# Regrouped first products, a second carrier for the sample-row writes, and waits with other releasers, in a two-layer decode step

## The chip, the cores and the metric

The kernel runs on one core of one Trainium2 chip. The metric is the device time of one execution in microseconds (us). TensorE (PE) multiplies and transposes, VectorE (DVE), ScalarE (ACT) and GpSimd (POOL) work on what it makes, and SyncE (SP) issues most transfers. ACT and POOL can issue transfers too, each on a queue of its own.

## What is computed

The reference is one inference step of a decoder with two layers. 512 new rows of a prompt and 64 rows of samples (8 sequences of 8 tokens) go through a convolution layer, one projection to keys and values, and a sparse-attention layer.

```python
def conformer_layer(x, conv_prev, g_pre, w_in, conv_w, conv_b, ln_g, ln_b, w_out, g_post):
    h = rms_norm(x, g_pre)
    a, b, z = jnp.split(h @ w_in, 3, axis=-1)
    glu = a * jax.nn.sigmoid(b)
    full = jnp.concatenate([conv_prev.astype(glu.dtype), glu], axis=1)
    c = lax.conv_general_dilated(full, ...) + conv_b
    y = jax.nn.silu(layer_norm(c, ln_g, ln_b)) * jax.nn.silu(z)
    return x + rms_norm(y @ w_out, g_post), full[:, -(CONV_W - 1):]
...
    cmp_p, slc_p, win_p = kv_rows(xp, kv_norm, w_kv)
    kc_p, vc_p, ks_p, vs_p = sparse_keys(cmp_p, slc_p, cmp_pe, cmp_w1, cmp_w2)
    win_all = jnp.concatenate([state_win.astype(win_s.dtype), win_s], axis=1)
...
        xp = nsa_output(xp, op, zp, gp, b_w_out[l], b_norm_post[l])
```

D_MODEL is 1024, there are 16 heads of 64, 4 key/value heads and three branches: compressed keys, selected blocks, and a window. Besides the rows of both layers the kernel returns the new states. Two of them are mostly copies of an input: the last 30 rows that enter the convolution for each sample (22 old ones, 8 new ones) and the window of each sample (256 old rows, 8 new ones).

## The kernel before, in words

Each engine has a program of its own, written out by hand in the order in which it runs. They meet by counting semaphores: then_inc adds to one when an instruction or a transfer is done, wait_ge holds the engine that reaches it. Nothing is reordered, so what stands behind a wait waits too. A transfer adds 16 when it has landed.

All large products are made in three parts, because fp32r keeps fewer bits than the data: high part times high part, low weights times high rows, and high weights times low rows. tile_hi and tile_lo are the parts of a weight tile; ACT copies the high one (line L842 for every copy), DVE or POOL subtract to get the low one.

The stages, with their place in the span:

- **Start, 0 to 30 us.** Five blocks of rows are normalised and transposed by turn_a(t) (L2034) and split into h_hi and h_lo (DVE L1385). keep_busy(n) (L2039) issues transposes whose result nobody reads. first_half(c, hf) makes the product of weight tile c with one half of the rows, 24 matmuls (L2097 to L2099). first_half(0, 0) waits for the low part of three row blocks (hl_ready 3) and of tile 0 (lo_pool 1).
- **Convolution layer, to 300 us.** Eight steps m make three tiles each. compress passes (L2090) are laid between; in one of them a product with ones sums the squares (L2089). DVE and POOL do the convolution of the samples. Then come the transposes of the new conv rows (L2173), the products with the output weights (first_rows L1984, split_out L2203 to L2205), and turn_b(t) (L2199), which transposes the normalised rows xn_b(t) of the next layer.
- **Around L777 to L779.** POOL writes bias_copies to memory in four transfers, then copies the old conv rows and the old window rows straight from input to output. ACT (L1033) writes the eight samples' new conv rows from conv_out_s, whose place in the arena kvh_whole takes over later. That is why DVE waits for them ahead of L1597.
- **Keys, values and queries, to 436 us, and attention, to 758 us.** Attention has 16 steps n. In each DVE sums eight units (sums, L1796), ACT takes exponentials (L1287), DVE takes reciprocals (den_of, L1805 and L1806), POOL scales (L823), PE transposes the probabilities (turns, L2424) and multiplies them with the values (L2454). The compressed branch has the same chain on a smaller table (den_of_cmp on DVE, L1780 to L1784; probs_cmp on POOL, L806). y_product (L1816) multiplies a result with its gate and frees its bank in PSUM. next_lo (L1656) makes the low part of the next weight tile.
- **Samples and output, from 758 us.** Sample attention, and pieces of the output product (L2494) laid between its steps. halves_at says which pieces go with which step. The last product is that of the sample rows (L2587), followed by its squares (ACT L1357), their sum (PE L2592), a scaling and an addition (DVE L1972, L1974).

Of the kernel before, what the change touches and what calls it, by code (L numbers as in the profile page):

```python
# [23 lines left out]
ALU = mybir.AluOpType  # L24
# [3 lines left out]
P = 128  # L28
# [39 lines left out]
def build(nc, I, O):  # L68
    ctx = ExitStack()
    with ctx:  # L70
# [166 lines left out]
        pts = at(R_G + 8192, 2, 3, P)  # L237
        vnew = at(R_G + 8960, 6, CH, p1=DS)
# [41 lines left out]
        def sem(name):  # L280
# [8 lines left out]
            co_tr co_ready co_out new_packed late  # L289
# [10 lines left out]
        ZEROED = {"slot": 1, "blocks": 3, "bias": 4, "pad": 5, "probs": 6, "table": 7, "queries": 8}  # L300
# [214 lines left out]
        def den_cmp(m):  # L515

            return 5 * m + 1

        def den_unit(n, g):

            return 2 * n + g + 1 + n // 2 + 1
# [48 lines left out]
        def _(sp):  # L570
# [101 lines left out]
            def new_v_rows(n):  # L672
                b, br = n // 2, n % 2
                sp.dma_start(vnew[:, n % 6], v_sb[DS * b:DS * b + DS, br, 4, :]).then_inc(slot_in[n % 6], 16)
# [11 lines left out]
            for n in range(4):  # L686
                past_rows(n)
            sp.wait_ge(S["x1_out"], 16 * TT)
# [10 lines left out]
            for n in range(2 * DB):  # L699
# [4 lines left out]
                new_v_rows(n)  # L704
# [12 lines left out]
        def _(pool):  # L717
# [22 lines left out]
            first_scale_far(3)  # L740
            pool.wait_ge(S["xn_a_ready"], TT)
# [74 lines left out]
            probs_cmp(0)  # L816
            for n in range(N_STEPS):
                m, br = n // 2, 1 + n % 2
                for j, (i, half) in enumerate(UNITS):
                    pool.wait_ge(S["den_ready"], den_unit(n, j // 4))  # L820
# [5 lines left out]
                if br == 2 and m + 1 < KD:  # L826
                    probs_cmp(m + 1)
            y_sum(N_STEPS - 1)
# [11 lines left out]
        def _(act):  # L840
# [50 lines left out]
            first_hi(3)  # L891
# [3 lines left out]
            copy(xn_a[4][0:NS], x_first[0:NS, 4], rs[0:NS, 4:5]).then_inc(S["xn_a_ready"], 1)  # L895
            first_hi(4)
            act.wait_ge(S["early_mm"], 1)
            copy(line[:, 0:SEQ], pb(0, SEQ, p1=H), -1.0).then_inc(S["line_part"], 1)
            act.wait_ge(S["early_mm"], 2)
            copy(pe_sb, pb(1, 2, 16)).then_inc(S["line_part"], 1)  # L900
# [335 lines left out]
            for n in range(2):  # L1236
                z_copy(n, 2 + 4 * n)
# [117 lines left out]
            act.wait_ge(S["fo_mm"], TT)  # L1355
            act.wait_ge(S["sq_a"], TT + 4)
            nc.scalar.activation(junk_c[:, 0:D // 2], pb(4, D // 2), ACT.Square, accum_out=ss[:, 4:5]).then_inc(S["sq_a"], 1)  # L1357
# [7 lines left out]
            act.wait_ge(S["co_out"], 16 * (1 + DB))  # L1365
            act.wait_ge(S["late"], 16 * (2 + 2 * DB))
# [3 lines left out]
        def _(dve):  # L1370
# [52 lines left out]
            first_lo(1)  # L1423
            first_lo(2)
            first_mean(4)
            first_turn(3)
            first_scale(4)
            first_turn(4)
            first_lo(3)
            first_weight_lo(1)  # L1430
# [3 lines left out]
            first_turn(5)  # L1434
# [137 lines left out]
            for t in range(TT + 1):  # L1572
# [163 lines left out]
            dve.wait_ge(S["late"], 16 * (2 + 2 * DB))  # L1736
# [887 lines left out]
```

## Time and profile before

| what | value |
|---|---|
| median of 3 runs | 876.22 us (875.26 to 877.77) |
| profiled execution | 875.5 us, its span 873.7 us |
| PE busy | 849.5 us, 97% of the span |
| DVE, ACT, POOL busy | 546.9, 479.9, 308.3 us |
| granted TensorE clock, mean | 0.997 of full speed |

The span is the time from the first to the last instruction of the execution that the hardware profiler recorded. The time of the execution is a little longer.

### The profile page before, as it was taken

What the parts mean: (1) busy time and instruction counts of PE and PEld (TensorE: products, weight loads), DVE (VectorE), ACT (ScalarE), POOL (GpSimd) and SP (SyncE); (2) the same over time, 40 slices, a digit from 0 to 9 for tenths busy, and PEclk for the clock granted to TensorE, in tenths of its full rate; (3) what the DMA queues carried; (4) which work ended last, traced back from release to release, by engine and by line L of the source; (5) the groups of instructions that cost most, each with busy time, mean ns of one, the idle gap of its engine ahead of it and who ended that gap; (6) DMA issues with size and microseconds to landing.
All of it is one profiled execution on the core that took longest, in us unless ns stands there. A gap on an engine that the chain in (4) does not pass through costs nothing.

```text
span 873.7 us, 16552 instructions
## 1 busy us (share of the span) xinstructions
PE 849.5 (97%) x6246; PEld 761.8 (87%) x6246; DVE 546.9 (63%) x1179; ACT 479.9 (55%) x940; POOL 308.3 (35%) x311
## 2 busy tenths in 40 slices
PE   7999999999999999999988999999999999999996
PEld 6999999955887778889978999999999999987774
DVE  6579999998967683333255555655565645536674
ACT  6667776633742543334376666767667676524241
POOL 2399888879050000003022333334343433300000
PEclk9999999999999999999999999999999999999999
DMA  9465433127259465067321323232323322472621
GB/s 250 116 176 152 119 101 80 58 49 240 67 166 377 178 214 164 10 157 209 82 57 25 74 52 89 56 73 50 73 50 74 73 50 50 93 236 86 207 87 37
DMA packets 158164, 99.51 MB, mean 114 GB/s; under 512 B 97202, under 2 KB 147026, under 8 KB 158005
## 3 DMA queue, kind: packets, MB, share of 16 engines
q1 hardware_dynamic: 143278, 79.30, 33.8%
q0 software_dynamic: 4896, 10.32, 3.4%
q10 hardware_dynamic: 9911, 8.84, 3.1%
q8 instruction: 50, 0.82, 0.4%
q14 instruction: 29, 0.24, 0.1%
HBM read 89.58 MB, written 18.85 MB: 124 GB/s over the span
## 4 chain that ended last, share of the span: by engine, by line
PE 91%; DVE 4%; ACT 3%; issue 1%; ACTq 1%; POOL 0%; DVEq 0%
PE psum L2377 7%; PE psum L2378 7%; PE psum L2379 7%; PE psum L2494 6%; PE psum L2003 6%; PE psum L2005 6%; PE psum L2004 6%; PE psum L2090 5%; PE psum L2203 4%; PE psum L2454 4%; PE psum L2204 4%; PE psum L2205 4%; PE psum L2424 4%; PE psum L2410 3%; PE psum L1984 2%; PE psum L2566 2%
## 5 line engine op out<-in xcount | busy, mean ns | idle before, releaser
L842 ACT ACTIVATE arena<-psum 128x512 f32<-128x512 f32 (+7 forms) x211 | 92.1, 473 | 145.3 <-PE psum L2379 66.4
L2377 PE MATMUL psum<-u_hi,tile_hi 128*128 128x288 f32 x464 | 140.5, 303 | 0.0
L2378 PE MATMUL psum<-u_lo,tile_hi 128*128 128x288 f32 x464 | 137.6, 297 | 0.0
L823 POOL TENSOR_SCALAR arena<-arena,kept 128x512 f32<-128x512 f32 (+3 forms) x128 | 90.2, 725 | 134.1 <-DVE kept L1806 134.1
L2379 PE MATMUL psum<-u_hi,tile_lo 128*128 128x288 f32 x464 | 136.7, 295 | 0.0
L1468 DVE SCALAR_TENSOR_TENSOR psum<-arena,psum 128x512 f32<-128x512 f32 x168 | 127.0, 756 | 6.0
L2003 PE MATMUL psum<-h_hi,tile_hi 128*128 128x288 f32 x352 | 104.3, 296 | 0.0
L2004 PE MATMUL psum<-h_lo,tile_hi 128*128 128x288 f32 x352 | 103.8, 295 | 0.0
L2005 PE MATMUL psum<-h_hi,tile_lo 128*128 128x288 f32 x352 | 103.8, 295 | 0.0
L2377 PEld LDWEIGHTS psum<-u_hi,tile_hi 128*128 128x128 f32 x464 | 87.4, 188 | 3.0 <-issue 2.6
L2378 PEld LDWEIGHTS psum<-u_lo,tile_hi 128*128 128x128 f32 x464 | 87.4, 188 | 0.3
L2379 PEld LDWEIGHTS psum<-u_hi,tile_lo 128*128 128x128 f32 x464 | 87.1, 188 | 0.0
L1287 ACT ACTIVATE arena<-arena,kept 128x512 f32<-128x512 f32 (+3 forms) x128 | 70.0, 549 | 21.9 <-DVE kept L1796 21.9
L1656 DVE TENSOR_TENSOR tile_lo<-tile_whole,tile_hi 128x1024 fp32r<-128x1024 f32 x32 | 39.7, 1240 | 46.3 <-ACT tile_hi L842 46.3
L1796 DVE CUSTOM_DVE_ANT_0 arena<-psum,arena 128x512 f32<-128x512 f32 (+3 forms) x128 | 53.9, 487 | 21.9 <-PE psum L2410 21.9
L2004 PEld LDWEIGHTS psum<-h_lo,tile_hi 128*128 128x128 f32 x352 | 66.9, 190 | 0.0
L2003 PEld LDWEIGHTS psum<-h_hi,tile_hi 128*128 128x128 f32 x352 | 66.3, 188 | 0.0
L2005 PEld LDWEIGHTS psum<-h_hi,tile_lo 128*128 128x128 f32 x352 | 66.2, 188 | 0.0
L842 ACT ACTIVATE tile_hi<-tile_whole 128x1024 fp32r<-128x1024 f32 x56 | 58.9, 1052 | 5.6 <-PE psum L2005 5.5
L732 POOL TENSOR_TENSOR tile_lo<-tile_whole,tile_hi 128x1024 fp32r<-128x1024 f32 x22 | 53.4, 2429 | 21.0 <-ACT tile_hi L842 20.9
L2494 PE MATMUL psum<-arena 128*128 128x256 f32 x256 | 60.0, 381 | 0.0
L2090 PE MATMUL psum<-arena 128*128 128x495 f32 (+2 forms) x192 | 54.2, 441 | 0.9 <-ACT arena L842 0.9
(332 smaller groups left out, 1889.9 us busy)
## 6 DMA issues: line engine op xcount, KB each, us to landing
tile_whole<-in_b_w_in SPq DMA_DIRECT2D x64, 256.0 KB
tile_whole<-in_a_w_in SPq DMA_DIRECT2D x24, 512.0 KB
arena<-in_cmp_w SPq DMA_DIRECT2D x4, 2048.0 KB, 9.7
kvw_whole<-in_w_kv SPq DMA_DIRECT2D x6, 1024.0 KB, 14.7
bias_copies<-bias_line POOLq DMA_DIRECT2D x4, 1280.0 KB, 23.5
arena<-in_x_prompt SPq DMA_DIRECT2D x8, 512.0 KB, 6.4
kvw_whole<-in_a_w_out SPq DMA_DIRECT2D x4, 1024.0 KB, 11.4
arena<-bias_copies SPq DMA_DIRECT2D x16, 256.0 KB, 3.8
```

The source lines that it names most:

```text
L823: pool.tensor_scalar(L, L, rden[:, 8 + j:9 + j], gR[:, i, h:h + 1], ALU.mult, ALU.mult).then_inc(S["pn_ready"], 1)
L842: return nc.scalar.activation(out, in_, ACT.Copy, scale=scale)
L1287: nc.scalar.activation(L, L, ACT.Exp, scale=-1.0, bias=mn[:, 8 + j:9 + j], accum_out=den[:, 8 + j:9 + j]).then_inc(S["exp_done"], 1)
L1468: V.scalar_tensor_tensor(out=acc_p, in0=glu_p[:, m, w:w + SEQ], scalar=tap, in1=acc_p, op0=ALU.mult, op1=ALU.add).then_inc(S["conv_step"], 1)
L2003: pe.matmul(out, w_hi[:, k], h, start=(k == 0), stop=False)
L2004: pe.matmul(out, w_hi[:, k], l, start=False, stop=False)
L2005: ins = pe.matmul(out, w_lo[:, k], h, start=False, stop=(k == KD - 1))
L2090: ins = pe.matmul(pb(cs_bank(c, ht), 33, NCS)[:, seqs], w1[:, j, ht * P:(ht + 1) * P], ctS[:, j % 8, seqs, j // 8:j // 8 + NCS], start=(j ...
L2377: pe.matmul(pb(b, HT), w_hi, u_hi[:, k, here], start=(k == 0), stop=False)
L2378: pe.matmul(pb(b, HT), w_hi, u_lo[:, k, here], start=False, stop=False)
L2379: ins = pe.matmul(pb(b, HT), w_lo, u_hi[:, k, here], start=False, stop=(k == KD - 1))
L2494: ins = pe.matmul(pb(4 + 2 * (t % 2), 4, CH)[:, c], yT[:, k, t * P:(t + 1) * P], chunk_sb(C_OB + c)[:, k], start=(k == 0), stop=(k == KD - 1))
```

## The change

Six places are edited.

1. At the start two keep_busy calls go. first_half becomes first_third: the eight matmuls of one kind stand together, and each kind has its own wait. The transposes of the sample rows, turn_a(4), stand behind the first eight of tile 1. The low part of tile 1 is made by POOL instead of DVE, with a semaphore w1_lo.
2. In the compress pass the sum of squares stands at j = 10 instead of 6. The transposes of the conv rows stand ahead of the product for vc.
3. The eight writes of the new conv rows move from ACT's queue to POOL's, behind the copies of L777 to L779, and count in late, which the two state copies leave for page_in. DVE waits for late ahead of L1597.
4. In attention den_of_cmp(0) and probs_cmp(0) stand later, a small exponential is added between two copies of ACT, and y_product(m, 0) stands ahead of next_lo. The functions that count turns, scaled_unit and scaled_cmp, follow.
5. new_v_rows(0) to (3) are loaded earlier, behind two memsets of POOL (zeroes, 10), and the third value matmul takes 128 rows of weights instead of 8, the rest zero.
6. The pieces halves_at[0] stand between the first two steps. y_sample_sum(0) stands earlier. The last block is squared in two halves of 256 columns, multiplied with its gain before the mean is known, and finished by one operation.

```diff
@@ GpSimd
             first_scale_far(3)
+            pool.wait_ge(S["hi_ready"], 2)
+            pool.tensor_tensor(out=tile_lo[:, 1], in0=tile_w[:, 1], in1=tile_hi[:, 1], op=ALU.subtract).then_inc(S["w1_lo"], 1)
...
             pool.wait_ge(S["line_out"], 16)
+            pool.wait_ge(S["page_in"], 16)
             for h0 in range(0, H, 4):
                 pool.dma_start(bias_copies[h0:h0 + 4], bias_dram[h0:h0 + 4].unsqueeze(1).broadcast_to([4, P, NX])).then_inc(S["bias_out"], 16)
-            pool.dma_start(O["conv_sample"][0, :, 0:W - 1 - DS, :], I["state_conv"][0, :, DS:W - 1, :]).then_inc(S["late"], 16)
-            pool.dma_start(O["win_sample"][:, 0:PAST], I["state_win"]).then_inc(S["late"], 16)
-
+            pool.dma_start(O["conv_sample"][0, :, 0:W - 1 - DS, :], I["state_conv"][0, :, DS:W - 1, :]).then_inc(S["page_in"], 16)
+            pool.dma_start(O["win_sample"][:, 0:PAST], I["state_win"]).then_inc(S["page_in"], 16)
+
+            pool.wait_ge(S["co_ready"], 2)
+            for b in range(DB):
+                pool.dma_start(O["conv_sample"][0, b, W - 1 - DS:W - 1], conv_out_s[DS * b:DS * b + DS]).then_inc(S["late"], 16)
@@ ScalarE
             act.wait_ge(S["co_tr"], 2)
-            copy(conv_out_s[0:NS], pb(6, D, p1=NS)).then_inc(S["co_ready"], 1)
-            act.wait_ge(S["co_ready"], 2)
-            for b in range(DB):
-                act.dma_start(O["conv_sample"][0, b, W - 1 - DS:W - 1], conv_out_s[DS * b:DS * b + DS]).then_inc(S["co_out"], 16)
-
+            copy(conv_out_s[0:NS], pb(2, D, p1=NS)).then_inc(S["co_ready"], 1)
...
-            for n in range(2):
-                z_copy(n, 2 + 4 * n)
+            z_copy(0, 2)
+            nc.scalar.activation(sd[:, 6:7], ident[:, 0:1], ACT.Exp)
+            z_copy(1, 6)
@@ VectorE
                     if k == 0:
                         dve.wait_ge(S["y_ready"], KD)
-                        dve.wait_ge(S["co_out"], 16 * (1 + DB))
+                        dve.wait_ge(S["co_out"], 16)
+                        dve.wait_ge(S["late"], 16 * DB)
...
             sums_cmp(0)
-            den_of_cmp(0)
             for n in range(N_STEPS):
                 m, br = n // 2, 1 + n % 2
                 sums(n)
                 den_of(n, 0)
+                if n == 0:
+                    den_of_cmp(0)
...
-                next_lo(tile_over(n, 1))
                 if br == 1:
                     y_product(m, 0)
-                elif m + 1 < KD:
+                next_lo(tile_over(n, 1))
+                if br == 2 and m + 1 < KD:
@@ TensorE
-            for t in range(1, 3):
-                turn_a(t)
-                keep_busy(4)
+            turn_a(1)
+            keep_busy(4)
+            turn_a(2)
             small_tables()
             turn_a(3)
-            keep_busy(4)
...
-                    if squares and j == 6:
+                    if squares and j == 10:
...
+            def first_third(c, hf, part):
+
+                w, h = ((tile_hi, h_hi), (tile_hi, h_lo), (tile_lo, h_hi))[part]
+                last = 1 if hf or c == 0 else 2
                 for k in range(KD):
-                    out, here = pb((2, 0)[c] + hf, HT), slice(hf * HT, hf * HT + HT)
-                    pe.matmul(out, tile_hi[:, c, k], h_hi[:, k, here], start=(k == 0), stop=False)
-                    pe.matmul(out, tile_hi[:, c, k], h_lo[:, k, here], start=False, stop=False)
-                    ins = pe.matmul(out, tile_lo[:, c, k], h_hi[:, k, here], start=False, stop=(k == KD - 1))
+                    ins = pe.matmul(pb((2, 0)[c] + hf, HT), w[:, c, k], h[:, k, hf * HT:hf * HT + HT],
+                                    start=(part == 0 and k == 0), stop=(part == last and k == KD - 1))
                 return ins
...
+            pe.wait_ge(S["hh_ready"], 3)
+            pe.wait_ge(S["hi_ready"], 1)
+            first_third(0, 0, 0)
+            pe.wait_ge(S["lo_pool"], 1)
+            first_third(0, 0, 2)
             pe.wait_ge(S["hl_ready"], 3)
-            pe.wait_ge(S["lo_pool"], 1)
-            first_half(0, 0)
+            first_third(0, 0, 1)
...
+            pe.wait_ge(S["new_packed"], DB)
+            for k in range(KD):
+                ins = pe.transpose(pb(2, KD, P, p1=NS)[:, k], new_rows[:, k], ident)
+            ins.then_inc(S["co_tr"], 1)
             pe.wait_ge(S["hid_ready"], 4)
             pe.wait_ge(S["z_ready"], KD)
@@ the last block, VectorE
+            for c in range(2):
+                dve.wait_ge(S["sq_a"], 2 * TT + c)
+                n_dve[0] += 1
+                V.tensor_tensor(out=y_out[:, 0, c * CH:(c + 1) * CH], in0=pb(4 + c, CH), in1=gpost_s[:, c * CH:(c + 1) * CH],
+                                op=ALU.mult).then_inc(dve_step, 1)
```

On TensorE at the start, the end of the transposes and the first product with its filler stand in this order before (L2034 is turn_a, L2039 keep_busy, L2097 to L2099 the three kinds):

```order
L2034 MATMUL psum<-kept,arena 128x128 [waits h_ready,xn_a_ready]
L2034 MATMUL psum<-kept,arena 128x128 x7
L2039 MATMUL psum<-kept 128x128 x4
L2097 MATMUL psum<-h_hi,tile_hi 128x288 [waits lo_pool,hl_ready,vec_ready]
L2098 MATMUL psum<-h_lo,tile_hi 128x288
L2099 MATMUL psum<-h_hi,tile_lo 128x288
```

With the change, from the same transposes on (L2067 is turn_a, L2131 any product of first_third):

```order
L2067 MATMUL psum<-kept,arena 128x128 [waits h_ready,xn_a_ready]
L2067 MATMUL psum<-kept,arena 128x128 x7
L2131 MATMUL psum<-h_hi,tile_hi 128x288 [waits hi_ready,hh_ready,vec_ready]
L2131 MATMUL psum<-h_hi,tile_hi 128x288 x7
L2131 MATMUL psum<-h_hi,tile_lo 128x288 [waits lo_pool]
L2131 MATMUL psum<-h_hi,tile_lo 128x288 x7
L2131 MATMUL psum<-h_lo,tile_hi 128x288 [waits hl_ready]
L2131 MATMUL psum<-h_lo,tile_hi 128x288 x7
L2131 MATMUL psum<-h_hi,tile_hi 128x288 [waits hi_ready,line_part]
L2131 MATMUL psum<-h_hi,tile_hi 128x288 x7
L2067 MATMUL psum<-kept,arena 128x64 [waits h_ready,xn_a_ready]
```

The wait for low rows (hl_ready) stood at the first matmul and now stands at the seventeenth, and turn_a(4) has moved behind 32 products.

On GpSimd, behind the products of the sample convolution, before:

```order
L777 DMA bias_copies<-bias_line 512x1x640 [waits line_out]
L777 DMA bias_copies<-bias_line 512x1x640 x3
L778 DMA out_conv_sample<-in_state_conv 8x2x11264
L779 DMA out_win_sample<-in_state_win 8x8x16384
L784 MEMSET arena 128x512 [waits kv_ready,xn_b_ready,x1_out]
```

and with the change:

```order
L791 DMA bias_copies<-bias_line 512x1x640 [waits page_in,line_out]
L791 DMA bias_copies<-bias_line 512x1x640 x3
L792 DMA out_conv_sample<-in_state_conv 8x2x11264
L793 DMA out_win_sample<-in_state_win 8x8x16384
L797 DMA out_conv_sample<-arena 8x1024 [waits co_ready]
L797 DMA out_conv_sample<-arena 8x1024 x7
L801 MEMSET arena 128x512 [waits kv_ready,xn_b_ready,x1_out]
```

Eight small transfers have come behind the window copy on this queue.

On VectorE at the first step of attention, before (L1773 ends sums_cmp, L1780 to L1784 are den_of_cmp, L1796 begins sums(0)):

```order
L1773 TENSOR_TENSOR arena<-arena,kept 128x248 [waits dve_step]
L1780 TENSOR_REDUCE kept<-arena 128x8 [waits exp_done]
L1781 TENSOR_SCALAR kept<-kept 128x8 [waits dve_step]
L1782 RECIPROCAL kept<-kept 128x8 [waits dve_step]
L1784 TENSOR_TENSOR kept<-kept 128x8 [waits dve_step]
L1796 ISA arena,kept<-psum,arena 128x512 [waits s_done]
```

and with the change, the end of sums(0) and what follows (L1827 and L1828 are den_of, L1802 to L1806 den_of_cmp, L1678 next_lo):

```order
L1818 ISA arena,kept<-psum,arena 128x256 [waits s_done]
L1818 ISA kept 128x1
L1827 TENSOR_SCALAR kept<-kept 128x4 [waits exp_done]
L1828 RECIPROCAL kept<-kept 128x4 [waits dve_step]
L1802 TENSOR_REDUCE kept<-arena 128x8 [waits exp_done]
L1803 TENSOR_SCALAR kept<-kept 128x8 [waits dve_step]
L1804 RECIPROCAL kept<-kept 128x8 [waits dve_step]
L1806 TENSOR_TENSOR kept<-kept 128x8 [waits dve_step]
L1827 TENSOR_SCALAR kept<-kept 128x4 [waits exp_done]
L1828 RECIPROCAL kept<-kept 128x4 [waits dve_step]
L1678 TENSOR_TENSOR tile_lo<-tile_whole,tile_hi 128x1024 [waits hi_ready]
```

The four operations have moved from ahead of sums(0) to between its two groups of denominators.

## Rows read from the trace of the kernel before

**Rows 1.** The page's first part: busy us, share of the span, instructions.

```profile
PE 849.5 (97%) x6246; PEld 761.8 (87%) x6246; DVE 546.9 (63%) x1179; ACT 479.9 (55%) x940; POOL 308.3 (35%) x311
```

**Rows 2.** Waits of PE, whole span: releaser, us in total, times, longest.

```profile
PE psum L2089 <- DVE arena L1502: 1.4, 1, 1.4
PE psum L1984 <- ACT arena L935: 1.1, 2, 1.0
PE psum L2203 <- DVE kvw_rest L1527: 1.1, 1, 1.1
PE psum L2592 <- ACT arena L1357: 0.9, 1, 0.9
...
PE psum L2534 <- ACT arena L842: 0.8, 1, 0.8
PE psum L2587 <- issue: 0.8, 1, 0.8
```

**Rows 3.** Timeline of PE, 17 to 24 us: start, duration, line, operation, [idle before].

```profile
17.51 0.60 PE L2039 MATMUL psum<-kept 128*128 128x128 f32 x4
18.91 0.37 PE L2097 MATMUL psum<-h_hi,tile_hi 128*128 128x288 f32 x1 [0.80 <-issue]
...
22.26 0.71 PE L2034 MATMUL psum<-kept,arena 64*128 64x64 f32 x8
23.20 0.40 PE L2097 MATMUL psum<-h_hi,tile_hi 128*128 128x288 f32 x1 [0.24 <-ACT kept L842]
```

**Rows 4.** Timeline of DVE, 17 to 19 us.

```profile
17.26 1.55 DVE L1385 TENSOR_TENSOR h_lo<-h_whole,h_hi 128x1024 fp32r<-128x1024 f32 x2
```

**Rows 5.** Timeline of PE, 224 to 243 us.

```profile
224.90 17.97 PE L2090 MATMUL psum<-arena 128*128 128x240 f32 x84
```

**Rows 6.** Timeline of ACT, 249 to 257 us.

```profile
253.72 2.76 ACT L842 ACTIVATE y_hi<-y_whole 128x3072 fp32r<-128x3072 f32 x1 [4.14 <-issue]
```

**Rows 7.** Timeline of DVE, 256 to 288 us.

```profile
256.52 1.23 DVE L1522 TENSOR_TENSOR y_lo<-y_whole,y_hi 128x1024 fp32r<-128x1024 f32 x1 [8.02 <-ACT y_hi L842]
...
283.90 1.22 DVE L1597 TENSOR_TENSOR kvh_whole<-psum,arena 128x1024 f32<-128x1024 f32 x1
...
286.78 0.75 DVE L1607 TENSOR_SCALAR arena<-arena,kept 128x1024 f32<-128x1024 f32 x1
```

**Rows 8.** Timeline of PE, 290 to 291 us.

```profile
290.29 1.03 PE L2199 MATMUL psum<-kept,arena 128*128 128x128 f32 x8
```

**Rows 9.** Timeline of POOL, 248 to 254 us.

```profile
253.38 0.59 POOL L779 DMA_DIRECT2D out_win_sample<-in_state_win  x1
```

**Rows 10.** The tile out_win_sample (L779 once, L787 sixteen times): its transfers' landings.

```profile
DMA to landing us min/median/max: 3.2/5.2/46.2
```

**Rows 11.** The page's DMA issues: KB each, median us to landing.

```profile
out_conv_sample<-in_state_conv POOLq DMA_DIRECT2D x1, 704.0 KB, 29.6
```

**Rows 12.** Timeline of PE, 446 to 465 us.

```profile
449.31 1.41 PE L2424 MATMUL psum<-kept,arena 128*128 128x128 f32 x8 [2.76 <-POOL arena L823]
...
461.33 4.07 PE L2454 MATMUL psum<-arena 128*64 128x128 f32 x40 [2.86 <-DVE arena L1816]
```

**Rows 13.** Busy time by window; the column behind POOL is the granted clock.

```profile
462.00:464.00 2.00, 2.00 (x22) 2.00 (x20) 2.00 (x11) 2.00 (x6) 0.00 (x0) 0.50 0.00 0
```

**Rows 14.** The chain that ended last, one of fifteen like it: start, us, what.

```profile
483.51 2.33 PE psum L2454 x40
```

**Rows 15.** Timeline of DVE, 443 to 461 us.

```profile
443.54 0.41 DVE L1780 TENSOR_REDUCE kept<-arena 128x8 f32<-128x248 f32 x1 [1.59 <-ACT arena L1270]
...
444.52 0.68 DVE L1796 CUSTOM_DVE_ANT_0 arena<-psum,arena 128x512 f32<-128x512 f32 x1
...
459.45 1.23 DVE L1656 TENSOR_TENSOR tile_lo<-tile_whole,tile_hi 128x1024 fp32r<-128x1024 f32 x1 [3.50 <-ACT tile_hi L842]
460.60 0.68 DVE L1816 TENSOR_TENSOR arena<-psum,arena 128x512 f32<-128x512 f32 x1
```

**Rows 16.** Timeline of DVE, last 4 us.

```profile
869.82 0.69 DVE L1974 TENSOR_TENSOR arena<-arena 128x512 f32<-128x512 f32 x1
```

More of the change, by code:

```diff
@@ L298, in build @@
             """.split()}
-        ZEROED = {"slot": 1, "blocks": 3, "bias": 4, "pad": 5, "probs": 6, "table": 7, "queries": 8}
+        ZEROED = {"slot": 1, "blocks": 3, "bias": 4, "pad": 5, "probs": 6, "table": 7, "queries": 8, "rest": 10}
         w_in = [sem(f"w_in{i}") for i in range(RING)]
@@ L515, in den_cmp, with scaled_unit, scaled_cmp @@
         def den_cmp(m):
-            return 5 * m + 1
+            return 5 * m + (1 if m else 2)
+        def scaled_unit(n, j):
+            return unit_at(n, j) - (1 if n == 0 and j < 2 else 0)
+        def scaled_cmp(m):
+            return cmp_at(m) if m else 3
         def den_unit(n, g):
-            return 2 * n + g + 1 + n // 2 + 1
+            return 2 * n + g + 1 + n // 2 + (1 if n or g else 0)
         def turned(n, g):
@@ L687, in _ @@
                 past_rows(n)
+            sp.wait_ge(S["zeroes"], ZEROED["rest"])
+            for n in range(4):
+                new_v_rows(n)
             sp.wait_ge(S["x1_out"], 16 * TT)
@@ L890, in _ @@
             first_root(4)
-            first_hi(3)
+            act.wait_ge(S["early_mm"], 1)
+            copy(line[:, 0:SEQ], pb(0, SEQ, p1=H), -1.0).then_inc(S["line_part"], 1)
+            act.wait_ge(S["early_mm"], 2)
+            copy(pe_sb, pb(1, 2, 16)).then_inc(S["line_part"], 1)
             act.wait_ge(S["rs_a"], 2)
@@ L895, in _ @@
             copy(xn_a[4][0:NS], x_first[0:NS, 4], rs[0:NS, 4:5]).then_inc(S["xn_a_ready"], 1)
+            first_hi(3)
             first_hi(4)
[L897 to L900, printed above, removed]
             first_hi(5)
@@ L1956, in _ @@
                     last_sum(norm_at[w - 2])
-            dve.wait_ge(S["ys_mul"], 2 * DB * 3)
-            ys = yT[:, :, SEQ:NT]
-            for br in range(2):
-                V.tensor_tensor(out=ys, in0=ys, in1=y_br[:, br], op=ALU.add).then_inc(S["y_s"], 1)
-                dve.wait_ge(S["y_s"], br + 1)
+                if w == 2 * DB + 2:
+                    y_sample_sum(0)
+            y_sample_sum(1)
             last_mean(3)
@@ L2523, in _ @@
             LATE_CUTS = ((2, 4), (2, 4), (2, 3), (1, 4))
-            for h in halves_at[0]:
-                last_part(4 + h // 2, range(4 * (h % 2), 4 * (h % 2) + 4))
             for w in range(2 * DB + 4):
@@ L2543, in _ @@
                     pe.transpose(pb(3, P), orow[:, n % 2], ident).then_inc(S["ot_tr"], 1)
-                for h in halves_at.get(w, ()) if 0 < w < 2 * DB else ():
+                for h in halves_at.get(w, ()) if w < 2 * DB else ():
                     last_part(4 + h // 2, range(4 * (h % 2), 4 * (h % 2) + 4))
@@ L2586, in _ @@
                     for half in range(2):
-                        ins = pe.matmul(pb(4, 2, CH, p0=half * NS, p1=half * NS + NS)[:, c], yT[:, k, SEQ:NT],
+                        ins = pe.matmul(pb(4 + c, CH, p0=half * NS, p1=half * NS + NS), yT[:, k, SEQ:NT],
                                         chunk_sb(C_OB + 2 * half + c)[:, k], start=(k == 0), stop=(k == KD - 1))
+                ins.then_inc(S["fo_mm"], 1)
+            pe.wait_ge(S["ones_ready"], 3)
+            for c in range(2):
+                pe.wait_ge(S["sq_a"], 2 * TT + c)
+                ins = pe.matmul(pb(3, 1), fold, ss[:, 4 + c:5 + c], start=(c == 0), stop=(c == 1))
             ins.then_inc(S["fo_mm"], 1)
-            pe.wait_ge(S["ones_ready"], 3)
-            pe.wait_ge(S["sq_a"], 2 * TT)
-            pe.matmul(pb(5, 1), fold, ss[:, 4:5], start=True, stop=True).then_inc(S["fo_mm"], 1)
 INPUTS = ['x_prompt', 'x_sample', 'state_conv', 'cache_cmp', 'cache_slc', 'state_win', 'page_table', 'rel_bias',
```

87 lines of the change are left out of this document (50 added, 37 removed).

## The prediction

> **What bounds the kernel now.** The page's first part says it: TensorE (PE) is busy for 849.5 of 873.7 us [rows 1]. No other engine and no queue comes near, so a gain can only be idle time of PE that goes away, and a loss only idle time that is added. The view of PE's waits is therefore read second; the single waits that the diff touches are in it [rows 2]. The timelines of PE, VectorE (DVE), ScalarE (ACT) and GpSimd (POOL) around each say what released them [rows 3 to 9, 12, 15, 16]. The reader should see there that most of these waits are a microsecond or less, so that the sum of all that can be won is near 13 us of 24, and that one transfer lasts longer than that sum [rows 9, 10].
>
> The numbers below are places in the span of before, unless said otherwise. The profiled execution took 875.5 us (span 873.7 and 1.8 around it), 0.7 below the median of the three runs (876.22).
>
> **The change part by part.**
>
> *Start.* The first product stands at 18.91, held for low parts of the activations that DVE ends at 18.81 [rows 3, 4]. With the products grouped by kind, the first eight need high parts alone; PE can begin them where the removed filler matmuls stood, at 17.51 [rows 3]. 24 products take 3.3 us there (18.91 to 22.26). Up to the next group before: 23.20 plus 3.3, 26.5. After: 17.5 plus 48 products (6.6) plus the transposes (0.7 to 0.9 [rows 3]) is 24.7, and if DVE or POOL is late by a little, 25. The wait before 23.20 (0.24) goes too. The low part of weight tile 1 moves from DVE to POOL, which has nothing else then; eight high products, the transposes and eight more cover it. I take **−1.9** (bounds −1.0 and −2.2). The conv loop behind has no PE wait that the view lists, so it moves as a block. The filler matmuls kept PE busy; the clock would have to fall before this turned into a loss, and no stretch here shows that.
>
> *205 to 265 us.* The product of the squares stands four matmuls later in its pass: PE waited 1.4 for it [rows 2], and four matmuls of this pass take 1.7 (84 records in 17.97, two for each matmul [rows 5]), so **−1.4**. The transposes of the conv rows go ahead of the product that waited 1.0 for ACT [rows 2], and take as long: **−0.9**. ACT no longer issues eight small output DMAs: it lost 4.14 us before its copy y_hi [rows 6], DVE waited for that copy [rows 7], and PE waited 1.1 for DVE's kvw_rest behind it [rows 2]. PE comes 2.3 earlier and DVE's chain 4.1 earlier; so PE's wait becomes zero, **−1.1**, with a bound of zero if a reload that DVE needs further on comes late. Together −3.6 (−2.3 to −3.6). POOL issues the DMAs instead, for which no engine waits at the issue.
>
> *The landing of these DMAs.* The eight small DMAs now count in the semaphore late, and DVE waits for all eight before it overwrites their source, in the step that writes kvh_whole at 283.90 [rows 7]. Before, it waited for the same DMAs on ACT's own queue, where nothing stood ahead of them. Now they are issued on POOL's queue behind the four bias copies, the conv state copy and the window state copy. The window copy is issued at 253.38 [rows 9] and lands 46.2 us later [rows 10], at 299.6; the conv copy, issued 0.6 before it, lands 29.6 later [rows 11], at 282.4. POOL issues nothing else until later, so before shows no small DMA behind a large one. Bounds: nothing, if the small ones pass (the sixteen small window writes that POOL issues much later, with nothing large ahead, make the median landing of 5.2 [rows 10]; eight issues of 0.59 each [rows 9] behind 254 and such a landing would be done by 264), and the end of the window copy, 299.6, if each engine's share of the queue is served in order. I take the second, since the landings of this queue follow the order of issue: 282.4 for the one, 299.6 for the next.
> Queued behind DVE's wait is all of its step: two writes, two small operations, and xn_b(1), which ends at 287.53, so 3.6 after 283.90 [rows 7]. PE's transposes at 290.29 [rows 8] need it. From 299.6 that gives 303.2 instead of 290.3: **+12.9**, which already contains that PE had come 3.6 earlier (that gain is lost in the wait, of some 16.5). Work on both engines behind it moves by the same. PE would stand idle for 16 us, and after its two waits of 2.8 and 2.9 at 449 and 461 [rows 12] the granted clock fell to 0.50 (1.2 GHz) in 462 to 464 [rows 13], so that a group of 40 records took 4.07 instead of 2.33 [rows 12, 14]. I add the same **+1.7**. Sum of this stage +14.6, with bounds +10 (window copy 4 us faster, since DMAs were taken from the contended stretch, and no clock loss) and +16 (the small ones land 1.5 after it).
> The Trainium skill, "DMA: Bandwidth & Descriptors", section "Queues, rings and completion order", states that each DMA engine has a ring of its own for each queue row and consumes descriptors in ring order; section "Why a DMA increments its semaphore by 16 and not by 1" has it that on this kind of queue all 16 engines post an increment whatever the shape. By these the small DMAs' last increments stand behind the window copy's last packet, and the sum is the forecast's; were the rule not to hold here, the sum would be that of the first rival. No row of before shows it for a small DMA.
>
> *Start of attention, n = 0.* DVE's den_of_cmp(0) waits 1.59 for ACT's exponential from 441.95, and its four operations hold sums(0) until 444.52 [rows 15]. Moved behind the sums and the first denominators, it stands in ACT's shadow; the sums start 2.5 earlier, and with them ACT's exponentials and POOL's scaling, on which PE waits 2.76 at 449.31 [rows 12]. I take 2.4 off that wait. PE's second wait, 2.86 at 461.33 [rows 12], is for y_product(0,0), which stands behind a low part at 459.45 to 460.60 [rows 15]; put ahead of it, it ends at about 456.4, 0.5 after PE comes to it, so 2.4 goes here too, and the slow stretch behind it, 1.7 [rows 12, 14], goes as well. Given back: sums(1) would start at 458.5, and 4.8 later (444.52 to 449.31) the turns of n = 1 can go, 463.3; PE is there at 456.4 plus 2.4 plus 3.3, 462.1, so a new wait of 1.2. That is −2.4 − 2.4 − 1.7 + 1.2 = **−5.3** (−3.5, if the table load or the new wait costs more, to −6.6).
>
> *Tail.* The 16 records that now stand between two transposes cover the wait of 0.8; the earlier sum of the sample rows takes the other 0.8 [rows 2] down to nothing: −1.5. At the very end one DVE operation of 0.69 [rows 16] goes, and half of the square lies under the product, some 0.2: −0.9. POOL's two memsets and the wider third value product (8 rows of weights to 128, same count) lie in POOL's free time at the end of attention. **−2.4** (−1.5 to −2.8).
>
> Sum: −1.9 + 14.6 − 5.3 − 2.4 = +5.0 on 875.5, so 880.5, and with the 0.7 to the median **881 us**. Its own range is 876 to 886.
>
> **The rivals.**
> *First, faster: the small DMAs do not wait for the window copy.* For it: nothing in before shows a small one behind a large one, and DVE's need comes late: they have until 283.1 (286.7, where PE would be, less 3.6). Against it: the landings in order of issue [rows 10, 11]. It gives −1.9 − 3.6 − 5.3 − 2.4 = −13.2: 862.3, median 863. The point that decides is 283.1 for the eighth landing.
> *Second, they land with the conv copy or the end of the bias copies.* 282.4 [rows 11] plus up to 5: the loss is 0 to 4 of the 13.2: 863 to 867. For it: the window copy may use only part of the DMA engines.
> *Third, the stall and less of the gains.* The start gives 1.0, attention 3.5, the tail 1.5, and the stage of the landing loses its 16: 875.5 + 16 − 6.0 = 885.5, median 886.
> *Fourth, no change that can be told:* the stall at its lower bound, +10, with the gains of the other stages whole (9.6): 875.9, median 876.6.
>
> **How the numbers follow.** A measurement of this kernel tells 0.3% (2.6 us) from no change, so below 873.6 is faster and above 878.8 slower. Stall as forecast or larger (third rival with it) 0.60; stall near its lower bound, between the two limits, 0.19; first rival 0.13; second 0.05; stall so short that the time is under 873.6, 0.03. Faster 0.21, same 0.19, slower 0.60. Leaving out 0.1 above 885.5 and 0.1 at the fast end puts the range at 862.5 to 885.5: both signs are in it.
>
> **What would show it.** First product at about 17.5; no wait for the squares; ACT's y_hi right behind the conv copy, near 249.6; at about 300 on DVE a wait before the line that writes kvh_whole of 15 us or more, put down to late's DMAs, and on PE a wait of 14 to 17 before the transposes that follow, with a slow clock behind; the eight small DMAs with landings of 40 us and more. In attention PE's first wait near 0.4, the 40 records at 2.4. If the eight landings are short, the prediction falls as a whole, to the first rival; if they are long and DVE's wait is there but PE's is less than 10, my reading of what is queued behind DVE is wrong.

## The result, and the profile after

The change makes the kernel slower: 883.57 us, median of 4 runs (883.44 to 883.77), against 876.5 (875.26 to 877.77). The ratio is 1.0081, with a 95% interval of 1.0063 to 1.0098. The forecast was 881 in a range of 862.5 to 885.5, which reaches from clearly faster to clearly slower. The profiled execution took 883.4, with a span of 881.6.

The page's first part, answering to [rows 1]:

```profile
PE 848.9 (96%) x6240; PEld 763.3 (87%) x6240; DVE 548.3 (62%) x1179; ACT 479.9 (54%) x943; POOL 316.9 (36%) x322
```

PE works as long as before, within 0.6 us. The span grew by 7.9, so the loss is idle time, or slow clock, which counts as busy. PE's waits, answering to [rows 2] (releaser, us in total, times, longest):

```profile
PE psum L2241 <- DVE arena L1629: 18.1, 1, 18.1
PE psum L2072 <- POOL kept L732: 1.6, 1, 1.6
PE psum L2466 <- POOL arena L841: 1.6, 2, 1.3
PE psum L2131 <- DVE h_lo L1407: 1.2, 1, 1.2
...
PE psum L2634 <- ACT arena L1377: 0.3, 1, 0.3
```

The waits for the squares and for kvw_rest are gone. Of the tail's three waits one is left, with 0.3. In attention the wait of 2.8 has shrunk to 0.3 and the one of 2.9 is gone. Two small ones are new, 1.3 at the next step of attention and 1.2 at the start, and a large one of 18.1. What releases it stands on VectorE, where [rows 7] had no such wait (timeline of DVE, 280 to 306):

```profile
280.19 1.23 DVE L1608 TENSOR_TENSOR arena<-arena 128x1024 f32<-128x1024 f32 x1
302.22 1.22 DVE L1619 TENSOR_TENSOR kvh_whole<-psum,arena 128x1024 f32<-128x1024 f32 x1 [20.81 <-DMA out_conv_sample<-arena]
...
305.10 0.75 DVE L1629 TENSOR_SCALAR arena<-arena,kept 128x1024 f32<-128x1024 f32 x1
```

The chain that ended last (start, us, what) passes over the same transfer. It is the longest piece of the whole chain:

```profile
250.75 3.24 POOL bias_copies L791 x3
...
255.13 3.56 POOL out_conv_sample L797 x7
258.69 43.34 DMA out_conv_sample<-arena
...
306.00 1.94 PE psum L2241 x8
```

The last of eight writes of 32 KB each is issued at 258.69 and counted 43.3 later, at 302.03. The window copy was issued at 254.55 (timeline of POOL) and its answer by tile gives, as [rows 10] before:

```profile
DMA to landing us min/median/max: 3.4/5.2/45.6
```

so it landed at 300.15, and the last of the small writes 1.9 behind it. The trace's own list of packets on POOL's queue shows why. The data packets of the small writes (4096 bytes) were all started before 285. The 4-byte packets come in two groups, and the second, from 296.9 to 300.8, runs while the last of the window's packets (65536 bytes) end: the last one started at 297.1 and took 2.4 (packets by the microsecond in which they started, bytes: count; some lines left out):

```
281.0  4: 45   4096: 26   45056: 1   65536: 5
...
283.0  4: 20   4096: 10              65536: 3
284.0  4: 4    4096: 3               65536: 4
...
290.0                                65536: 3
...
295.0                                65536: 3
...
297.0  4: 20                         65536: 1
298.0  4: 43
...
300.0  4: 34
```

The increments of late say the same. Eight writes make 128 of them. 64 had come by 285.6, none came in the next 12 us, and the other 64 came from 297.6 to 302.03. All data packets had been started by then, and DVE waited 17 us more to be told so. (The view of landings gives these writes 26.6, 28.9 and 43.3 as least, median and most. All eight count in one semaphore, so it takes the first 64 increments for four whole landings.)

The Trainium skill, "DMA: Bandwidth & Descriptors", section "Why a DMA increments its semaphore by 16 and not by 1", says of this kind of queue that all 16 engines post an increment, whatever the shape of the transfer. The trace agrees: a write of 8 data packets made 16 increments, and half of them stood behind the window copy.

The stretch behind the wait ran at half clock. In the windows below the column behind POOL is the granted clock, 0.50 being 1.2 GHz. PE had done nothing for 18 us.

```profile
284.00:288.00 4.00, 3.89 (x17) 2.81 (x15) 0.00 (x0) 0.00 (x0) 0.00 (x0) 1.00 0.53 228
288.00:302.00 14.00, 0.00 (x0) 0.00 (x0) 0.00 (x0) 0.00 (x0) 0.00 (x0) 0.59 0.44 179
302.00:306.00 4.00, 0.00 (x0) 0.03 (x1) 3.48 (x6) 1.31 (x2) 0.00 (x0) 0.50 0.01 3
306.00:310.00 4.00, 4.00 (x14) 3.52 (x15) 1.14 (x3) 3.09 (x10) 0.00 (x0) 0.50 0.00 0
310.00:314.00 4.00, 4.00 (x17) 3.17 (x16) 2.26 (x5) 2.32 (x4) 0.00 (x0) 0.86 0.00 0
```

The start did not gain either. Timeline of PE, to be read against [rows 3]:

```profile
17.42 2.17 PE L2131 MATMUL psum<-h_hi,tile_hi 128*128 128x288 f32 x8
19.39 1.93 PE L2131 MATMUL psum<-h_hi,tile_lo 128*128 128x288 f32 x8
21.16 1.22 PE L2131 MATMUL psum<-h_lo,tile_hi 128*128 128x288 f32 x8
...
29.65 1.33 PE L2131 MATMUL psum<-h_lo,tile_hi 128*128 128x288 f32 x8 [1.15 <-DVE h_lo L1407]
```

The first product begins at 17.42 as forecast, but eight matmuls take 2.2 and 1.9 instead of 1.2, and a new wait of 1.15 follows. The clock in this stretch:

```profile
18.00:20.00 2.00, 2.00 (x10) 2.00 (x10) 2.00 (x6) 1.49 (x5) 1.29 (x1) 0.50 1.09 225
```

Places that both traces have give the account. Each is the start of the same work after, less before.

| place | shift, us | this stage |
|---|---|---|
| second transposes of the conv state, 29.67 before | +1.15 | start +1.15 |
| turn_b(1), 290.29 before | +15.71 | |
| turn_b(2), 302.32 before | +18.12 | 205 to 302: +17.0 |
| values of n = 1 in attention, 483.51 before | +13.0 | attention −5.1 |
| last product, 860.02 before | +9.0 | |
| end of the span | +7.9 | tail −5.1 |

### The profile page after: what moved, and what is told of

Its sections match the earlier page's. It is cut to its first block, busy times and chain, and to the rows that moved or that the text cites. A ratio compares the mean times of both kernels' runs of the same rounds, so it can differ in the third digit from the quotient of the medians.

```text
span 881.6 us, 16552 instructions
## 1 busy us (share of the span) xinstructions
PE 848.9 (96%) x6240; PEld 763.3 (87%) x6240; DVE 548.3 (62%) x1179; ACT 479.9 (54%) x943; POOL 316.9 (36%) x322
## 4 chain that ended last, share of the span: by engine, by line
PE 84%; DMA 5%; DVE 5%; ACT 2%; POOL 2%; issue 1%; ACTq 1%; DVEq 0%; POOLq 0%
PE psum L2419 7%; PE psum L2420 7%; PE psum L2421 7%; PE psum L2536 6%; PE psum L2036 6%; PE psum L2037 6%; PE psum L2038 6%; DMA out_conv_sample<-arena 5%; PE psum L2496 4%; PE psum L2466 4%; PE psum L2245 4%; PE psum L2246 4%; PE psum L2247 4%; PE psum L2452 3%; PE psum L2122 3%; PE psum L2017 2%
## 5 line engine op out<-in xcount | busy, mean ns | idle before, releaser
L1678 DVE TENSOR_TENSOR tile_lo<-tile_whole,tile_hi 128x1024 fp32r<-128x1024 f32 x32 | 39.2, 1227 | 38.1 <-ACT tile_hi L864 38.1
## 6 DMA issues: line engine op xcount, KB each, us to landing
kvw_whole<-in_w_kv SPq DMA_DIRECT2D x6, 1024.0 KB, 14.6
```

## The experiments

Each kernel is the changed one with the edit shown, unless said otherwise. All medians are of 4 runs. Before took 876.54 beside the first four, 876.58 beside the next four, and 875.84 beside the last three.

| kernel | median us | ratio to before, 95% interval |
|---|---|---|
| small_first | 862.59 | 0.9845 (0.9827 to 0.9864) |
| win_behind | 866.80 | 0.9898 (0.9878 to 0.9917) |
| keep_mid | 882.00 | 1.0059 (1.0043 to 1.0076) |
| k8 | 885.24 | 1.0095 (1.0078 to 1.0112) |
| move_only | 893.89 | 1.0198 (1.0179 to 1.0218) |
| small_on_act | 864.73 | 0.9876 (0.9854 to 0.9897) |
| sf_keep | 861.26 | 0.983 (0.9814 to 0.9847) |
| combo | 859.79 | 0.9813 (0.9796 to 0.9829) |
| combo_att | 865.41 | 0.988 (0.9864 to 0.9897) |
| combo_y | 862.51 | 0.9845 (0.9828 to 0.9861) |
| combo_k64 | 862.18 | 0.9841 (0.9825 to 0.9858) |

**small_first: the eight writes ahead of everything on the queue.**

```diff
+            pool.wait_ge(S["co_ready"], 2)
+            for b in range(DB):
+                pool.dma_start(O["conv_sample"][0, b, W - 1 - DS:W - 1], conv_out_s[DS * b:DS * b + DS]).then_inc(S["late"], 16)
             for h0 in range(0, H, 4):
                 pool.dma_start(bias_copies[h0:h0 + 4], ...)
...
-            pool.wait_ge(S["co_ready"], 2)
-            for b in range(DB):
-                pool.dma_start(O["conv_sample"][0, b, W - 1 - DS:W - 1], conv_out_s[DS * b:DS * b + DS]).then_inc(S["late"], 16)
```

> The changed kernel with the eight small writes of new conv rows issued by POOL ahead of the four bias copies and the two state copies, all else kept. Theory (on each DMA engine the queue is served in order, so the last increments of the small writes stand behind the window copy's packets): with nothing large ahead the eight land within 6 us of their issue, DVE's wait of 20.8 before the write of kvh_whole is gone, PE's wait of 18.1 too and the slow clock behind it (2.4); since PE also gets back what the earlier edits gave, the time is 20 to 21 us below the changed kernel: 863. Rival (the landings are long because this stretch is crowded, whatever the order): they take 20 us and more here too, and the time is above 875. Rival (DVE waits for something else by then): PE's wait stays above 5 us.

It took 862.59, 21.0 below the changed kernel. The writes landed like this:

```profile
DMA to landing us min/median/max: 2.0/2.0/2.4
```

No wait of PE for DVE at turn_b is left in its waits. The order of eight issues decides 21 us. Here the writes were done by 254.1, before the first window packet started (280.0), so this run alone does not tell the order from the crowd; the increments above and the next run do. Two of the four executions took 861.2 and two 864.0; sf_keep comes back to that.

**win_behind: only the window copy goes behind them.**

```diff
-            pool.dma_start(O["win_sample"][:, 0:PAST], I["state_win"]).then_inc(S["page_in"], 16)
-
             pool.wait_ge(S["co_ready"], 2)
             for b in range(DB):
                 pool.dma_start(O["conv_sample"][0, b, W - 1 - DS:W - 1], conv_out_s[DS * b:DS * b + DS]).then_inc(S["late"], 16)
+            pool.dma_start(O["win_sample"][:, 0:PAST], I["state_win"]).then_inc(S["page_in"], 16)
```

> The changed kernel with the window copy alone issued behind the eight small writes; bias copies and conv state copy stay ahead of them. Theory (order in the queue, and the window copy is what counts): in the changed kernel the small writes' own packets were all moved by 285, and only some increments came after the window's last packet. So the eight land at 282 to 285 here, DVE's wait falls from 20.8 to 1 to 4, PE's from 18.1 to 0 to 1.5, and the time is 863 to 865. Rival (the sum of bytes ahead counts, not which copy): 30% of the bytes ahead go with the window copy's 4 MB of about 10, so the wait falls by less than half and the time is 872 to 878.

It took 866.80, 1.8 above the range expected, and on the theory's side. In the profiled execution 1.8 of the distance to small_first is the clock at the start, which fell here (the second transposes of the conv state begin at 30.95, there at 29.18). DVE waits as the theory says, though a little longer:

```profile
286.54 1.23 DVE L1619 TENSOR_TENSOR kvh_whole<-psum,arena 128x1024 f32<-128x1024 f32 x1 [4.66 <-DMA out_conv_sample<-arena]
```

The landing at 286.4 is behind the conv copy and bias packets still ahead. The window's packets ran all the while (277.5 to 301.1) and did not hold the small writes up from behind. PE waits 2.0 and 0.5. What counts is that the window copy stands ahead: one transfer less ahead gives back 16.8 of the 21.

**move_only: this part alone, on the kernel before.** Only the eight writes and their semaphores are changed, as in part 3 of the change; conv_out_s still comes from its old bank.

```diff
-            act.wait_ge(S["co_ready"], 2)
-            for b in range(DB):
-                act.dma_start(O["conv_sample"][0, b, W - 1 - DS:W - 1], conv_out_s[DS * b:DS * b + DS]).then_inc(S["co_out"], 16)
...
+            pool.wait_ge(S["co_ready"], 2)
+            for b in range(DB):
+                pool.dma_start(O["conv_sample"][0, b, W - 1 - DS:W - 1], conv_out_s[DS * b:DS * b + DS]).then_inc(S["late"], 16)
...
```

> The kernel before with one part of the change alone: the eight small writes move from ACT's queue to POOL's, behind bias copies, conv state copy and window copy, and the semaphores follow; nothing else. Theory (the stall is this part's own doing): the last of the eight lands near 300 to 301, DVE waits for it some 19 us before the write of kvh_whole, PE 14 to 15, with 2.4 of slow clock behind. The time is 15 to 17 us above before: 892 to 894. Rival (the stall needs the other edits too, which move the place where DVE waits): less than 8 above before.

It took 893.89, 17.3 above before. PE's wait is there without any other edit:

```profile
306.28 1.94 PE L2201 MATMUL psum<-kept,arena 128*128 128x128 f32 x8 [17.47 <-DVE arena L1609]
```

It starts at 306.28, where the changed kernel starts at 306.00. In move_only the window copy was issued at 253.08 and landed 47.4 later, in the changed kernel at 254.55 and 45.6 later: 300.5 and 300.15, and before 299.6. So small shifts of its issue do not show at its end, and what is gained ahead of it in the program is lost in the wait.

**small_on_act: the eight writes back on ACT's queue.** The removed lines of move_only's diff stand again behind the copy of conv_out_s, and DVE waits for co_out.

> The changed kernel with the eight small writes back on ACT's queue, where they were, all else kept. Theory: no stall; ACT loses 4.1 again before y_hi, DVE's chain is 4 later, and PE waits about 1 to 2 for kvw_rest, since PE itself comes earlier than in before; 863 to 865, that is 1 to 2.5 above the kernel with the small writes first on POOL's queue. Rival (leaving ACT is what makes room, also further on): 866 or more.

It took 864.73, 2.1 above small_first and 18.8 below the changed kernel. ACT lost 3.07 at its issues, and PE waited 0.8 for kvw_rest. The 2.1 is not the price of the move alone: in this profiled execution the clock fell at the start (0.50 in 18 to 20), in that of small_first it did not. Counted from behind the start, from the second transposes of the conv state to turn_b(1), the stage took 258.2 here and 256.9 in small_first. So moving the writes off ACT was worth 1.3, near the 1.1 forecast, and cost 21 by where they were put.

**keep_mid: one filler put back.**

```diff
             turn_a(2)
+            keep_busy(4)
             small_tables()
```

> The changed kernel with one of the two removed fillers, the four transposes behind turn_a(2), put back; the one ahead of the first product stays out. Theory (the granted clock fell to 0.50 in 18 to 20 because PE did less ahead of the first product): the clock stays at 1.00, the first eight products take 1.2 instead of 2.2, and the time is 2 to 3 us below the changed kernel: 881. Rival (the clock falls because PE meets its new waits, filler or not): the time stays at 883.6.

It took 882.00, 1.6 below the changed kernel, less than the 2 to 3 expected. The clock did as the theory says:

```profile
18.00:20.00 2.00, 2.00 (x17) 2.00 (x16) 2.00 (x6) 1.49 (x5) 1.30 (x1) 1.00 1.13 228
```

The transposes of the conv state moved from 30.82 to 29.28, so the start gave 1.54, and PE's wait at turn_b grew from 18.1 to 19.4: of what the start gave, the stall took 1.3. turn_b(1) came only 0.29 earlier, as the last landing did (301.74 for 302.03). This profiled execution is 0.9 shorter than the changed kernel's; the other 0.7 arose behind the wait, where the slow clock ended sooner (turn_b(2) 13.75 behind turn_b(1), there 14.44).

**sf_keep: the same filler, on small_first.**

> The kernel with the small writes first, plus the one filler behind turn_a(2). With the small writes first alone, two executions of four took 861.2 and two 864.0, and the profiled one (861.1) kept the clock at 1.00 at the start where the changed kernel had 0.50. Theory (without the filler the clock at the start is at its edge: it falls in some executions and costs 2.8): with the filler all executions lie within 0.5 of 861.2. Rival (the two levels come from something else): two levels again, 2.8 apart.

All four executions took 860.85 to 861.32. Without the filler small_first had two levels, 2.8 apart, and its profiled one at the lower level had the clock at 1.00 in 18 to 20. The profiled executions of all kernels show the pattern. Without this filler the clock was at 0.50 in 18 to 20 in four of five (changed kernel, k8, win_behind, small_on_act; not small_first). With it, it was at 1.00 in all eight. So the removal of the fillers made the clock's fall at the start likely, and the one filler in a gap where PE was idle anyway is enough against it. A fall at the start cost 1.5 to 1.8 where it was traced; what the rest of the 2.8 is, no trace of a slower execution shows.

**combo: sf_keep, with POOL's subtraction behind DVE's.**

```diff
+            pool.wait_ge(S["hl_ready"], 5)
             for j in range(2, 5):
                 split_lo_a(j)
```

> As the one before, and POOL waits at the start until DVE has made the last low part of the rows, before it subtracts for weight tile 2. Theory (DVE's 128x512 subtraction took 2.87 instead of 0.69 because POOL's subtraction of 2.54 ran beside it): DVE's takes 0.7, PE's wait of 1.15 before the third group of the second half goes, and the time is 0.8 to 1.2 lower: 860. Rival (it is slow for its own reasons, or the transfers of the start crowd it): it still takes over 2, and the time is the same or, since POOL is later, higher.

It took 859.79 (859.62 to 859.94), 1.5 below sf_keep, a little more than expected, and the fastest of all, 0.9813 of before. In the changed kernel DVE and POOL read like this:

```profile
26.73 2.87 DVE L1407 TENSOR_TENSOR h_lo<-h_whole,h_hi 128x512 fp32r<-128x512 f32 x1
...
26.50 2.54 POOL L743 TENSOR_TENSOR tile_lo<-tile_whole,tile_hi 128x1024 fp32r<-128x1024 f32 x1 [5.17 <-ACT tile_hi L864]
```

and in combo:

```profile
25.20 0.68 DVE L1408 TENSOR_TENSOR h_lo<-h_whole,h_hi 128x512 fp32r<-128x512 f32 x1
...
25.96 2.39 POOL L743 TENSOR_TENSOR tile_lo<-tile_whole,tile_hi 128x1024 fp32r<-128x1024 f32 x1 [4.61 <-DVE h_lo L1408]
```

POOL's ended at 29.04 and DVE's 0.56 later, about the length of DVE's own work. This looks as if DVE did not go slower beside POOL but stood still until POOL was done. The Trainium skill, "SBUF — State Buffer", section "Who interferes with whom", says that a VectorE instruction with two inputs in SBUF contends with a GpSimd instruction that reads SBUF, and that the sharing of their ports is an exclusive lock. The rows agree (2.87 against 0.68).

**combo_att: attention as before.** Orders, counts and the small exponential of part 4 are undone on combo.

> The fastest kernel so far (small writes first, filler back, POOL behind DVE at the start: 859.8) with the whole attention edit undone: order of den_of_cmp(0) and probs_cmp(0), the small exponential, and the place of y_product, with their counts. Theory (the prediction's: the two waits of 2.8 and 2.9 and the slow clock behind them are worth 5 us): the time is 4.8 to 5.5 higher, 865. Rival (most of it would be hidden): less than 3 higher.

It took 865.41, 5.6 above combo, and the two waits of [rows 12] are back with 2.7 and 2.9. The profiled execution's span is 4.8 above combo's. Its 40 records behind the second wait took 2.40, at full clock. The slow stretch stood behind the first wait instead, which ended at 443.76:

```profile
446.00:448.00 2.00, 2.00 (x10) 2.00 (x10) 1.97 (x4) 1.97 (x3) 2.00 (x4) 0.50 0.00 0
```

**combo_y: only the place of y_product undone, on combo.**

```diff
-                if br == 1:
-                    y_product(m, 0)
                 next_lo(tile_over(n, 1))
+                if br == 1:
+                    y_product(m, 0)
```

> The same kernel with only the place of y_product(m, 0) undone, behind the next low part as in before. Theory: PE waits about 2.9 for it again at n = 0, since the low part behind which it stands waits for ACT; with one long wait instead of two the clock stays at 1.00, so the slow stretch of 1.7 does not come back, and part of the wait is taken from the one that follows at n = 1 (1.3): 1.5 to 2.9 higher, 861.3 to 862.7. Rival (one such wait is enough for the clock to fall): 4 higher or more, 864.

It took 862.51 (860.98 to 863.79), 2.7 above combo, in the range expected. The wait is back, and the clock fell, though for less long than in [rows 12]:

```profile
453.33 3.50 PE L2498 MATMUL psum<-arena 128*64 128x128 f32 x40 [2.86 <-DVE arena L1839]
```

In combo the same 40 records took 2.40 at 450.67, and a wait of 1.26 followed that combo_y does not have. 2.86 + 1.10 − 1.26 = 2.7. By places, attention up to n = 1 takes 2.6 longer. The expectation that the clock stays at 1.00 was wrong in the profiled execution.

**k8 and combo_k64: the height of the third value product.** With 8 rows as before, on the changed kernel, and with 64 on combo:

```diff
-                            weights = pts[:, n % 2, j, rows_p]
+                            weights = pts[:, n % 2, j, rows_p] if j < 2 else pts[0:64, n % 2, 2, rows_p]
-                            held = ... if j < 2 else vnew[:, n % 6, cols_p]
+                            held = ... if j < 2 else vnew[0:64, n % 6, cols_p]
```

> The changed kernel with the third value product of the sample attention back at 8 rows of weights instead of 128; memsets and the early loads of the new rows stay. Theory (the two narrow matmuls of each step cost 0.15 us more than two full ones, 16 steps): the time is 2.4 us above the changed kernel, 886.0, and a step is 4.15 long again instead of 4.00. Rival (the steps got shorter through the moved pieces or loads): the time stays within 0.5 of 883.6.

It took 885.24, only 1.7 above the changed kernel where 2.4 was expected, with executions from 884.18 to 886.04. The two profiled executions, 885.8 and 883.4, are 2.4 apart: their traces agree within 0.1 up to n = 1 in attention, and the last product begins 2.3 later.

> The same kernel with 64 rows instead of 128 in the third value product (the rest of the two buffers is not read). With 8 rows a step was 0.15 longer than with 128. Theory (what costs is that the height of the weights changes between neighbouring matmuls): 64 costs about as much as 8, and the time is 2.0 to 2.6 higher, 862. Rival (what costs is the small number of rows itself): 64 is as good as 128, 859.8.

It took 862.18 (862.16 to 862.32), 2.4 above combo. 64 rows cost what 8 cost. One step's twelve records with 128 rows (combo), and with 64 (combo_k64):

```profile
816.05 0.82 PE L2609 MATMUL psum<-arena 128*64 128x128 f32 x12
```

```profile
817.20 0.97 PE L2609 MATMUL psum<-arena 128*64 128x128 f32 x12
```

The matmuls move the same columns. In combo each pair of records starts 0.11 behind the pair before it. In combo_k64 the first pair with 64 rows starts 0.21 behind its full neighbour and the second 0.16 behind the first, and k8 has the same numbers with 8 rows. So the small number of rows is not what costs. Whether it is the change of height between neighbours, or any height under 128, these runs do not tell: they have no stretch where all neighbours are short.

## Why the prediction was right, and where its numbers were off

**The stall, right in kind and place.** It named the transfer, the queue, the wait on DVE, the wait on PE behind it and the slow clock. move_only, small_first and win_behind each confirm it.

**The closeness of the total, partly luck.** 881 was 2.6 short. The stall and the start together were 5.4 short, the tail gave 2.7 more than forecast, and the two errors cancel in part.

**Its size was short, in four terms.** Start and this stage together were forecast at −1.9 + 14.6 = +12.7 and measured +18.1. The window copy's end, 299.6, was taken as the end of the small writes; their increments came 1.9 behind it, and it ended 0.5 later itself: 2.4. DVE's chain and the handover took 0.4 more than 3.6. The slow clock cost 2.4, not 1.7, the value read from a shorter group of attention. And the step "it moves as a block" was wrong for a landing: whatever the start had gained would have moved DVE's and POOL's issues, but not the end of the copy. The 1.9 could not be counted together with the stall. These four, 2.4, 0.4, 0.7 and 1.9, are the 5.4. keep_mid shows the last, as far as one profiled execution can.

**The start, wrong.** "The clock would have to fall before this turned into a loss, and no stretch here shows that" was the failed step. It fell, for the price of 1.5 (keep_mid), and DVE's last low part, now later, stood beside POOL's subtraction, at 1.4 (30.03 to 28.62 for the same product, from keep_mid to combo). With both put right (combo) the product behind the second transposes of the conv state begins at 28.62 where before had 30.42: −1.8, what the grouping was forecast to give.

**205 to 265 us, right but hidden.** Of the three waits two are gone in the waits after, and 0.2 of the third is left. Their 3.6 was lost in the stall, as the prediction said, and shows in small_first: from the second transposes of the conv state to turn_b(1) it takes 3.7 less than before.

**Attention, right.** −5.1 against −5.3. The first wait fell from 2.76 to 0.30, the second vanished, 40 records took 2.40, and the wait at n = 1 is 1.26, forecast 1.2. combo_y prices the second step alone. Behind which of the two waits the clock falls differs between executions: in combo_att it was the first.

**The tail, mis-sized.** −5.1 against −2.4. The forecast terms measured about −1.0, −0.7 and −1.1, close to 0.8, 0.8 and 0.9. The rest, 2.4, came from the wider third product, which the prediction costed at nothing because its count stayed (k8, combo_k64).

**The first rival** priced the change without the stall at 863. small_first, where the small writes don't wait, took 862.6. Here too errors cancel: in its profiled execution (861.1) the start gave 0.5 for 1.9, the next stage 3.7, attention 5.2 and the tail 5.1 for 2.4.

## What to carry to other kernels

A small transfer whose end somebody waits for belongs ahead of the large ones on a queue, or on another queue: its data may be gone long before its semaphore says so. Where a fixed event like the end of a large copy sets a stage, gains ahead of it must not be added to the sum. An engine's idle gap may be carrying something, here the filler that kept the clock up, so look at what an added or removed instruction does to the clock and to the engine that shares a port, not only to the wait that it ends.

## What the runs showed of the hardware that was not expected

Matmuls with fewer weight rows, standing among matmuls with 128, cost time, and 64 rows cost as much as 8: 0.15 us per step for a group of four records among eight of 128, 2.4 us over 16 steps. Padding the short product with zeros to full height was faster. The Trainium skill, "TensorEngine Tiling (Array Packing)", section "Key Properties", says that changing the tiling mode drains TensorE. That the lower number of rows is such a change would fit, but no run here shows it.

Half of the increments of the small writes stood behind the large copy although their data did not: 64 of 128 came by 285.6, the rest from 297.6 on, and all data packets had been started before 285.

Without the filler the clock falls at the start in some executions and not in others (four of five profiled ones). What decides it in an execution stays open; no run here was made to tell.
